# Gate and up products of a Macaron transformer: five of 22 tile pairs per feed-forward block formed from seven block products instead of eight

## What is computed

```python
def swiglu(u, w_gate, w_up, w_down):
    return (jax.nn.silu(u @ w_gate) * (u @ w_up)) @ w_down
...
    for l in range(DEPTH):
        f = swiglu(rms_norm(h, ffn1_pre_g[l]), ffn1_w_gate[l], ffn1_w_up[l], ffn1_w_down[l])
        h = h + 0.5 * rms_norm(f, ffn1_post_g[l])
...
        h = h + rms_norm(y, mix_post_g[l])
        f = swiglu(rms_norm(h, ffn2_pre_g[l]), ffn2_w_gate[l], ffn2_w_up[l], ffn2_w_down[l])
        h = h + 0.5 * rms_norm(f, ffn2_post_g[l])
    return h[:, N_META:]
```

## Time and profile before

| | |
|---|---|
| time, median of 3 runs (lowest, highest) | 2030.61 us (2030.28, 2030.77) |
| profiled execution: its time, its span | 2030.33 us, 2028.5 us |
| TensorE busy | 2014.0 us, 99% of the span, 15084 matmuls |
| VectorE busy | 697.2 us, 34% |
| ScalarE busy | 747.9 us, 37% |
| GpSimd busy | 997.4 us, 49% |
| weight and activation loads | 173.40 MB, 26.1% of the 16 DMA engines' span |

### The profile page before, as it was taken

How to read it: one execution, slowest core, us unless ns; L and a number is a source line. 1 busy time by engine, 2 the same in 40 slices (tenths; PEclk the granted TensorE clock), 3 DMA queues, 4 the chain that set the end, 5 groups by cost and what they waited for, 6 DMA issues and landing times.

```text
span 2028.5 us, 37353 instructions
## 1 busy us (share of the span) xinstructions
PE 2014.0 (99%) x15084; PEld 1927.0 (95%) x15084; DVE 697.2 (34%) x1093; ACT 747.9 (37%) x1210; POOL 997.4 (49%) x1257
## 2 busy tenths in 40 slices
PE   9999999999999999999999999999999999999998
PEld 8999999999899999999999999999998998888887
DVE  6222210378546222210062222103885462222102
ACT  5222222455556222232252222223555462232221
POOL 3544454475315544454374444544853155554542
PEclk9999999999999999999999999999999999999999
DMA  4322332222101322232122323321222013323321
GB/s 175 103 85 92 98 111 83 69 94 79 63 32 45 106 89 93 85 125 88 57 94 84 93 87 100 113 84 58 96 84 67 32 53 104 97 92 111 114 72 42
DMA packets 48415, 174.85 MB, mean 86 GB/s; under 512 B 5184, under 2 KB 9408, under 8 KB 48320
## 3 DMA queue, kind: packets, MB, share of 16 engines
q1 hardware_dynamic: 48176, 173.40, 26.1%
q10 hardware_dynamic: 144, 0.10, 0.0%
HBM read 171.38 MB, written 2.10 MB: 86 GB/s over the span
## 4 chain that ended last, share of the span: by engine, by line
PE 98%; DVE 1%; ACT 0%; DMA 0%; issue 0%; SPq 0%; DVEq 0%
PE ps L1588 97%; PE ps L1927 1%; DMA h<-in_x 0%; DVE osb L1535 0%; DVE xl L1545 0%; DVE tail_step L1205 0%; PE ps L1806 0%; ACT xh L778 0%; DVE probT L1503 0%; ACT prob L1061 0%; DVE small L1512 0%; DVE h L1210 0%; ACT tmp L1097 0%; ACT xh L1112 0%; DVE wlo L1239 0%
## 5 line engine op out<-in xcount | busy, mean ns | idle before, releaser
L683 POOL TENSOR_TENSOR wlo<-raw,whi 128x256 fp32r<-128x256 f32 (+2 forms) x1148 | 911.9, 826 | 787.4 <-ACT whi L748 787.4
L1588 PE MATMUL ps<-xh,whi 128*128 128x264 f32 (+2 forms) x3000 | 706.1, 298 | 3.2 <-DVE xl L1244 1.3
L1588 PE MATMUL ps<-xl,whi 128*128 128x264 f32 (+2 forms) x3000 | 703.0, 297 | 0.0
L1588 PE MATMUL ps<-xh,wlo 128*128 128x264 f32 (+2 forms) x3000 | 701.6, 297 | 0.0
L1588 PEld LDWEIGHTS ps<-xh,whi 128*128 128x128 f32 x3000 | 489.1, 188 | 21.0 <-DVE wlo L1239 2.3
L1588 PEld LDWEIGHTS ps<-xl,whi 128*128 128x128 f32 x3000 | 487.8, 188 | 14.8
L1588 PEld LDWEIGHTS ps<-xh,wlo 128*128 128x128 f32 x3000 | 487.5, 188 | 14.0
L748 ACT ACTIVATE whi<-raw 128x1024 fp32r<-128x1024 f32 (+2 forms) x289 | 321.4, 1114 | 152.5 <-PE ps L1588 152.4
L1588 PE MATMUL ps<-hidh,whi 128*128 128x264 f32 (+2 forms) x1276 | 313.6, 296 | 0.0
L1588 PE MATMUL ps<-hidh,wlo 128*128 128x264 f32 (+2 forms) x1276 | 312.3, 295 | 0.0
L1588 PE MATMUL ps<-hidl,whi 128*128 128x264 f32 (+2 forms) x1276 | 312.3, 295 | 0.0
(11 more groups left out here) (192 smaller groups left out, 1685.9 us busy)
## 6 DMA issues: line engine op xcount, KB each, us to landing
raw<-in_ffn_up SPq DMA_DIRECT2D x88, 512.0 KB, 3.5
raw<-in_ffn_down SPq DMA_DIRECT2D x64, 704.0 KB, 4.1
raw<-in_ffn_gate SPq DMA_DIRECT2D x87, 512.0 KB, 3.5
raw<-in_w_in SPq DMA_DIRECT2D x28, 512.0 KB, 3.5
raw<-in_w_out SPq DMA_DIRECT2D x16, 512.0 KB, 3.5
raw<-in_w_q SPq DMA_DIRECT2D x8, 384.0 KB, 3.3
out_t<-h SPq DMA_DIRECT2D x16, 128.0 KB, 1.7
h<-in_x SPq DMA_DIRECT2D x2, 528.0 KB, 5.1
```

The lines of the kernel that those rows point to most:

```text
L683: ins = nc.gpsimd.tensor_tensor(w_lo(n)[:, at], raw[:, r, at], w_hi(n)[:, at].bitcast(F32), ALU.subtract)
L1588: return nc.tensor.matmul(o, w, x, start=start, stop=stop)
```

## The change

In the feed-forward blocks the pairs m = 5, 7, 9, 11 and 13 are made in another way. The gate tile over the up tile, each cut in two halves of 4 squares, is a 2x2 matrix of blocks; the activations, cut in channels 0 to 511 over 512 to 1023 and first over second half of the tokens, are another. The product of two such matrices needs 7 block products by Strassen's identity (Winograd's form) where the plain way needs 8, and additions: of weights (S1 to S4), of activations (T1 to T4), and of the products.

- A block product (`part`, inside `strassen`) is 4 squares by 3 matmuls on 264 tokens (256 in block 5) in one PSUM bank: 12 matmuls; a pair is 84 where it was 96 (48 wide ones in block 5).
- A pair has four weight tiles in the ring: gate; S1 and S3; S2 and the right half of up; S4 (512 columns). The second and fourth are not loaded, VectorE makes them in the raw slots (`sums`), and writes S2 over the left half of up. Their low halves are VectorE's too (`low`), those of the other two stay GpSimd's.
- The four activation sums are made once per block, 4 steps k of 2 chunks each: ScalarE copies two chunks with the norm's gain (`sum_inputs`), VectorE does four additions (`t_sums`), ScalarE rounds (`sum_hi`), VectorE makes the low half (`t_low`), during pairs 0 to 4.
- A third pair of PSUM banks is taken (unit z). ScalarE copies the first product out of it (`part_copy`), and VectorE joins the seven with seven additions of 264 columns (`strassen_sums`).
- The loops of the feed-forward blocks, and of the loads of `w_out`, are written out. The decay rates of the recurrence move from pair 0 to pair 18 of block 0.

```diff
+STRASSEN = (5, 7, 9, 11, 13)
@@ sync
+        def raw_reusable(eng, n):
+            if n >= RING:
+                wait_lo(eng, n - RING)
+                if KIND.get(n - RING) in ("gate", "s2up"):
+                    eng.wait_ge(w_sums, 3 * STRASSEN_N[n - RING] + 3)
-                sp.wait_ge(lo_ready, n + 1 + adv)
+                raw_reusable(sp, n)
@@ scalar, ffn
+                for m in range(FC):
+                    n = TILES_OF[b, m]
+                    if m in STRASSEN:
+                        part_copy(m)
+                        for i in range(3):
+                            hi(n[i] + RING)
+                        silu(m)
+                        hi(n[3] + RING)
+                        hid_hi(m)
+                        continue
+                    silu(m)
+                    if m:
+                        hi(n[0] + RING)
...
+                    hid_hi(m)
+                    hi(n[1] + RING)
@@ vector, ffn
+                def strassen_sums(m, part):
...
+                    if part == 0:
+                        dve.wait_ge(part_copied, q + 1)
+                        dve.wait_ge(slots_used, slot_used(n[0]))
+                        nc.vector.tensor_tensor(c11, x, c11, ALU.add).then_inc(part_added, 1)
+                    elif part == 1:
...
+                        nc.vector.tensor_tensor(x, x, bank(z, trim, 1), ALU.add).then_inc(part_added, 1)
...
+                        nc.vector.tensor_tensor(y, x, bank(z, trim, 0), ALU.add).then_inc(psum_free[pair_of(z)], 1)
...
+                        nc.vector.tensor_tensor(x, x, c22, ALU.add).then_inc(part_added, 1)
...
+                        nc.vector.tensor_tensor(c22, y, c22, ALU.add).then_inc(part_added, 1)
+                    elif part == 2:
+                        dve.wait_ge(slots_used, slot_used(n[2]))
+                        nc.vector.tensor_tensor(c21, y, c21, ALU.add).then_inc(part_added, 1)
+                    else:
+                        dve.wait_ge(slots_used, slot_used(n[3]))
+                        nc.vector.tensor_tensor(c12, x, c12, ALU.add).then_inc(part_added, 1)
@@ tensor
+            def strassen(b, m, trim, following):
...
+                slot_in(n[0])
+                part(n[0], False, tokens(0, a0), bank(z, trim, 0), ug).then_inc(part_mm, 1)
+                part(n[0], True, tokens(1, a0), bank(ug, trim, 0), uu).then_inc(slots_used, 1)
+                slot_in(n[1])
+                pe.wait_ge(t_lo_ready, KH * (b // 3 * 2 + b % 3 // 2) + KH)
+                part(n[1], False, sums(0), bank(uu, trim, 1))
+                pe.wait_ge(part_copied, q + 1)
+                part(n[1], True, sums(2), bank(z, trim, 0)).then_inc(slots_used, 1)
+                slot_in(n[2])
+                part(n[2], False, sums(1), bank(z, trim, 1)).then_inc(part_mm, 1)
+                part(n[2], True, sums(3), bank(uu, trim, 0)).then_inc(slots_used, 1)
+                slot_in(n[3])
+                part(n[3], False, tokens(1, a1), bank(ug, trim, 1), following).then_inc(slots_used, 1)
```

More of the change, by code:

```diff
@@ L146, in build_program @@
     U[NB, "post"] = n
+    GATE_U, UP_U, FIRST_U = {}, {}, {}
+    for b in range(NB):
+        if b % 3 != 1:
+            n = U[b, "gu"]
+            for m in range(FC):
+                FIRST_U[b, m] = n
+                n += m in STRASSEN
+                GATE_U[b, m], UP_U[b, m] = n, n + 1
+                n += 2
+            FIRST_U[b, FC] = n
     PAIR_OF, NTH = {}, {}
@@ L685, in lo @@
                 ins.then_inc(lo_ready, 1)
[L687 to L702, removed]
             def seam(b):
@@ L723, in _ @@
                     seam(b)
[L724 removed]
+                for n in range(slot0[b] + RING, slot0[b + 1] if b + 1 < NB else NSLOT):
+                    if n not in LO_DVE:
+                        lo(n)
             for i, k in enumerate(POOL_TAIL):
@@ new lines, in gate @@
+                def gate(m):
+                    ug = GATE_U[b, m]
+                    if m in STRASSEN:
+                        dve.wait_ge(part_added, 6 * STRASSEN_N[TILES_OF[b, m][0]] + 6)
+                    else:
+                        dve.wait_ge(slots_used, slot_used(TILES_OF[b, m][0]))
+                    nc.vector.tensor_tensor(halves(tmp[0], trim),
+                                            unit(ug, trim, trim and m > 1 and m not in STRASSEN),
+                                            halves(rs_in, trim), ALU.mult).then_inc(psum_free[pair_of(ug)], 1)
@@ new lines, in ffn @@
+                dve.wait_ge(rs_pre, 2 * (b + 1))
+                for m in range(FC):
+                    n = TILES_OF[b, m]
+                    nxt = [i + RING for i in n]
+                    sums(nxt[0])
+                    if m in STRASSEN:
+                        strassen_sums(m, 0)
+                        sums(nxt[1])
+                        low(nxt[0])
+                        sums(nxt[2])
+                        low(nxt[1])
+                        strassen_sums(m, 1)
+                        strassen_sums(m, 2)
+                        low(nxt[2])
+                        strassen_sums(m, 3)
+                        gate(m)
+                        up(m)
+                        sums(nxt[3])
+                        hid(m)
+                        low(nxt[3])
+                        hid_lo(m)
+                        continue
+                    gate(m)
+                    if m == 1:
+                        t_sums(0)
+                    elif 2 <= m <= 4:
+                        t_low(m - 1)
+                    sums(nxt[1])
+                    low(nxt[0])
+                    up(m)
+                    hid(m)
+                    low(nxt[1])
+                    hid_lo(m)
+                    if m == 1:
+                        t_low(0)
+                    if 1 <= m <= 3:
+                        t_sums(m)
+                    if b == 0 and m == FC - 4:
+                        decay_rates()
```

280 lines of the change are left out of this document (206 added, 74 removed).

## The result

The changed kernel takes 2001.28 us (median of 4 runs, 2001.12 to 2001.30) beside 2030.51 us of the kernel before (4 runs, 2030.28 to 2030.77): ratio 0.9856, interval 0.9839 to 0.9873. The gain is 29.2 us; the forecast was 29.4 and 2001.2 us.

A forecast was written before the change was run, and what follows sets the result against it. TensorE, busy 99%, was taken as the only bound: 15 pairs at 1.54 us (23.1) and five in block 5 (6.3) save 29.4 us, added work hidden, giving 2001.2 us against the median; range 1999.5 to 2008.5.

The forecast's parts named there:

- What bounds it: Whole kernel: TensorE busy 99% of the span, clock full at 2.4 GHz, no other resource ending anything.
- The term of the sum: TensorE per Strassen pair: 10.21 us, 1.54 less; in block 5 9.87 us, 1.25 less; 29.4 us in all.
- A start of each part at nothing: TensorE at each block product's start: a wait or new bank costs nothing where the wait is met.
- The rival of 22.4 us: TensorE: 7 x 20 part starts cost 0.16 us each, giving 2023.6 us; partial stalls of all kinds shared 0.13.
- Loops at nothing: Written-out feed-forward loops: cost nothing, since the openings of blocks are straight code and run no worse.
- activation sums at nothing: Pairs 1 to 4: VectorE gets 3.1 us and ScalarE 2.4 us more per pair, hidden in over 7 us free.
- VectorE's queue: After a Strassen pair's end S: work done at S+8.8, next up product due S+11.95, 3.1 us left (2.7 block 5).
- The copy: ScalarE's copy out of bank z: done at 3.5 us, fourth part starts at 4.37, 0.9 us to spare.
- The 0.4 us late that the rival assumed: Fourth part waits for the copy; with 0.16 restart 20 pairs lose 11 us: 2012; partial stalls of all kinds 0.13.
- Contention of VectorE and GpSimd: Eight SBUF-input VectorE instructions each wait w longer: 0.51 gives 2005.3 us, 0.25 no stall; partial stalls of all kinds 0.13.
- the rival, at 0.67 and more for each of eight instructions: VectorE blocked by GpSimd a full block each time, w 0.78: 2048.5 us, slower; w = 0.67 decides; chance 0.05.
- the two that I named: Tight places: VectorE's queue after a Strassen pair (3.1 us left) and the copy out of bank z (0.9 us).

The follow-up runs named there:

- the six pairs with S4 early: Changed kernel with Strassen pairs 5, 6, 8, 9, 11, 12 and S4 made right behind S2 where such pairs follow each other: 2019.62 us, ratio 0.9947.
- eight sums more: Changed kernel, its five pairs kept, with VectorE making S3 eight more times in each Strassen pair's preparation: 2076.24 us, ratio 1.0225.

## Why the prediction was right

- **What bounds it** held: 99% TensorE, full clock, no wait of TensorE in a Strassen pair.
- **The term of the sum**, 84 matmuls at 0.1215 for 96 at 0.1224, was 1.54 us a pair; measured are 1.51 (21.98 less 11.75 leaves 10.23 us for the pair, 10.21 forecast). In block 5 it was 1.25, measured 1.23 (21.01 less 11.12 leaves 9.89, forecast 9.87). The miss of 0.02 us a pair is within the pace of the two runs of the earlier trace rows from which it was taken: the pairs run at 0.1218, the slower of the two. The pairs thus brought 28.9 us of the 29.4, and the medians lie 29.2 apart; that the time came out within 0.1 us of 2001.2 is closer than the terms were, and in so far luck. An estimate from the figure of 2.5 ns over the columns (the Trainium skill, TensorE: Matmul & The Clock Gate, "Wait — 56ns, not 53.3ns?") would have given 2004.4 us; here the trace does not agree: a one-bank stream of 264 columns, each matmul with its own weight load, steps by 0.1218 us and not 0.1125, and the sum by rows was the nearer by 3 us.
- **A start of each part at nothing** held: 7 x 20 new starts and no long step. The rival of 22.4 us is out.
- **Loops at nothing** held (2030.61 without Strassen pairs), and so did the **activation sums at nothing** (one pair per block).
- **VectorE's queue**: forecast done at S+8.8 with 3.1 us left, measured S+8.6 and 3.38. Busy 913.9 us, forecast 901. Additions into PSUM took 0.44 us, priced at 0.42. The S3 sums and a part of the S1 sums were stretched (together some 11 us), and products beside GpSimd too. The largest excess is in the activation sums: priced at 0.42 us each, by a row with one input in PSUM, the 64 of them took 47.9 us and not 26.9. Beside GpSimd, which ran from 49.78 to 57.66, one took up to 0.97 us; at 64.91, while GpSimd stood idle, 0.43:

```profile
52.79 0.97 DVE L1430 TENSOR_TENSOR t_sum<-t_in,t_sum 128x264 f32<-128x264 f32 x1
...
64.91 0.43 DVE L1430 TENSOR_TENSOR t_sum<-t_in,t_sum 128x264 f32<-128x264 f32 x1
```

That busy time is only 13 us over the forecast has another reason: where VectorE works without a pause an instruction can start some 0.08 us before the one ahead of it ends, and busy time counts that once, where the forecast added up whole durations.

- **The copy**: forecast 0.9 us to spare, measured 1.27. The 0.4 us late that the rival assumed needed something more in front of it; with one more `hi` it is late, by 0.07 us, and the loss is 6.3 us.
- **Contention of VectorE and GpSimd** is there, but in the steady couples it met mainly one instruction. S3 takes 1.23 us and not 0.68, so w is 0.55 for one of eight instructions, against a margin of 4.0 us for all. By the rule of the Trainium skill (SBUF — State Buffer, "Who interferes with whom") the later of the two is blocked until the other ends. The trace agrees, for both sides: S1, 0.06 us ahead of GpSimd's subtraction, took 0.68 us and the subtraction 1.22 instead of 0.73, and S3, which came during the subtraction, was held until it ended. The three durations are the same in twelve couples, four in each of blocks 0, 2 and 3. Where GpSimd runs beside four sums in a row, in the six pairs with S4 early, the sums take 1.04 to 1.22 us and GpSimd's four subtractions 4.16 us together, where it needs 2.83 by itself. So a wait, when it comes, is most of a subtraction (0.55 of 0.73 us); the rival, at 0.67 and more for each of eight instructions, failed on how often they meet.

**What I had not seen** was that the tightest place is neither of the two that I named. "Both have over 7 us free in each pair" in pairs 1 to 4 counted busy time of before and left out the weight sums and low halves of the first Strassen pair, which fall into pairs 3 and 4 too; 0.87 us were left. It cost nothing in the change, and 7.4 us in the four first pairs when the queue was lengthened by some 2 us. The **restart** was mis-sized as well: I took 0.16 us, and the rows of the early-S4 run show 0.27 beyond the idle time (0.66 less 0.39). The first matmul behind a wait lasts 0.39 us instead of 0.28, which is the missing 0.11. That this is its weight load, no longer hidden, is my reading and wasn't tried by itself.

Open is how much of the six pairs' remaining loss (18 us over the change) would go with a fifth raw slot; I did not try it. VectorE's waits for the load of up are down to 9.0 us there, which speaks for a part only.

## What to carry to other kernels

When one engine is busy 99% in a steady stream, work that comes off it counts at the pace of the nearest same-shaped run in the trace, and work added elsewhere counts nothing, as long as each queue's order, written out in time against its due points, leaves room. Write that order out for the first occurrence too, where preparation and steady work overlap, because that is where the room was smallest. A margin in busy share over the whole span says little: nine pairs in a row left VectorE at 50% of the span, which was 76% in the stretch of the pairs, and cost 4%, by my reading through a loop of loads, sums and slots.

## What the hardware showed beyond what I expected

- Matmuls of 264 columns that alternate between two PSUM banks, two in a row with the same weights, step by 0.1224 us; when the same products stay in one bank for all squares, they step by 0.1218, which is 0.5% and 4.1 us over the kernel. Whether the banks or the order of weights and tokens make it was not tried.
- A wait of TensorE that is met 0.07 us late costs 0.23 us, and one with 0.39 us idle costs 0.66, so about 0.27 us comes on top once the array has run empty. In the runs with eight sums more and with nine pairs the granted clock also fell to its lower level for 3.4 us and more at a time, the first times behind idle times of TensorE of 1.89 and 1.27 us, and a matmul stepped by 0.22 us then.
- A VectorE instruction with both inputs in SBUF and a GpSimd subtraction held each other up: the sum took 1.23 us instead of 0.68 when GpSimd's had begun first, and GpSimd's took 1.22 instead of 0.73 when the sum had. An addition with one input in PSUM was not held up (0.43 to 0.44 us).
